# Router logits with the weights stationary: two 64-column halves and a product with unit matrices

## The reference

```python
xt = rmsnorm(h, norm2_g)
g_logits = xt @ w_rg + b_rg                 # 4 groups
g_w, g_idx = top_k(softmax(g_logits), 1)
e_logits = (xt @ w_rexp + b_rexp).reshape(-1, 4, 8)
e_w, e_idx = top_k(softmax(e_logits[group g_idx]), 2)
# every row is then sent to its two experts of 32 (gate, up, down) and the results are added to h
```

## Time and profile before

| what | value |
|---|---|
| median of 3 timed runs | 782.52 us |
| lowest and highest | 781.94 and 783.98 us |
| span of the profiled execution, first to last instruction | 783.6 us |
| busy share of PE, PEld | 95%, 74% |
| busy share of DVE, ACT, POOL | 52%, 33%, 9% |
| bytes read, written | 176.17 MB, 21.41 MB |
| mean granted clock of TensorE | 0.990 |

### The profile page before, as it was taken

One profiled execution on the slowest core, in us unless ns is written; L12 is line 12 of the kernel. 1 busy time (PEld: TensorE's weight loads), 2 busy tenths in 40 slices (PEclk: granted clock), 3 DMA queues, 4 the chain that ended last, 5 costly groups with the idle time before them and its releaser, 6 DMA issues.

```text
span 783.6 us, 12757 instructions
## 1 busy us (share of the span) xinstructions
PE 741.4 (95%) x5288; PEld 576.0 (74%) x5288; DVE 408.8 (52%) x755; ACT 259.2 (33%) x446; POOL 74.4 (9%) x104
## 2 busy tenths in 40 slices
PE   8999999999999999999999999999999997778884
PEld 7999999999999777899999988885333332323322
DVE  6999839986347785665154386554112111114226
ACT  5662351123486645532442341230111111100113
POOL 0100022001011111000000000011121221111100
PEclk9999999999999999999999999999999999999997
DMA  9578326434238433400260694389999999999994
GB/s 342 202 264 316 109 82 106 118 115 151 102 131 323 162 138 118 182 1 2 108 219 12 222 425 189 128 353 345 419 423 424 418 424 424 419 423 425 422 388 161
DMA packets 38143, 190.68 MB, mean 243 GB/s; under 512 B 5914, under 2 KB 7466, under 8 KB 21864
## 3 DMA queue, kind: packets, MB, share of 16 engines
q1 hardware_dynamic: 23696, 148.22, 47.8%
q0 software_dynamic: 11200, 34.98, 13.4%
q10 hardware_dynamic: 3184, 6.60, 2.3%
HBM read 176.17 MB, written 21.41 MB: 252 GB/s over the span
## 4 chain that ended last, share of the span: by engine, by line
PE 76%; DMA 14%; DVE 5%; ACT 3%; issue 1%; SPq 1%; DVEq 0%; ACTq 0%; POOLq 0%
PE ps L662 72%; DMA sb<-in_wexp 11%; PE ps L676 4%; DMA expert_rows<-sb 2%; DVE sb L2763 1%; DMA sb<-expert_rows 1%; DMA sb<-in_xT 1%; DVE sb L2298 1%; DVE sb L2284 1%; SPq L562 1%; ACT sb L1431 1%; ACT sb L1631 1%; DVE sb L2696 0%; ACT sb L1653 0%; ACT sb L1636 0%
## 5 line engine op out<-in xcount | busy, mean ns | idle before, releaser
L662 PE MATMUL ps<-sr 128*128 128x288 f32 (+3 forms) x2906 | 407.3, 300 | 3.5 <-DVE ps L2701 3.0
L662 PEld LDWEIGHTS ps<-sr 128*128 128x128 f32 (+1 forms) x2906 | 388.1, 188 | 18.6 <-issue 5.6
L662 PE MATMUL ps<-sb 128*64 128x512 f32 (+16 forms) x1984 | 296.9, 429 | 28.7 <-DMA sb<-in_wexp 18.1
L662 PEld LDWEIGHTS ps<-sb 128*64 128x64 f32 (+7 forms) x1984 | 148.0, 148 | 149.8 <-issue 124.7
L2632 DVE SCALAR_TENSOR_TENSOR sb<-sb,ps 128x256 f32<-128x256 f32 x16 | 6.7, 421 | 117.7 <-ACT sb L1830 117.7
L676 PEld LDWEIGHTS ps<-sb 128*128 128x128 f32 (+3 forms) x398 | 42.2, 140 | 31.0 <-issue 28.6
L676 PE MATMUL ps<-sb 128*128 128x128 f32 (+3 forms) x398 | 53.7, 273 | 2.3 <-issue 1.4
L2246 DVE TENSOR_TENSOR sr<-sb,sr 128x2048 fp32r<-128x2048 f32 (+1 forms) x17 | 39.3, 2320 | 29.1 <-ACT sr L1545 19.0
L2640 DVE COPY sb<-ps 128x1024 f32<-128x1024 f32 x15 | 18.4, 1225 | 54.5 <-PE ps L662 54.5
L1431 ACT ACTIVATE sb<-ps 128x576 f32<-128x576 f32 (+3 forms) x28 | 21.9, 783 | 67.4 <-PE ps L662 47.4
L2357 DVE SCALAR_TENSOR_TENSOR sb<-sb,ps 128x576 f32<-128x576 f32 x24 | 18.1, 753 | 46.5 <-PE ps L662 46.3
(11 more groups left out here) (291 smaller groups left out, 509.2 us busy)
## 6 DMA issues: line engine op xcount, KB each, us to landing
sb<-in_wexp SPq DMA_DIRECT2D x91, 1024.0 KB, 22.1
sb<-in_wstream SPq DMA_DIRECT2D x33, 1024.0 KB, 5.7
expert_rows<-sb ACTq DMA_DIRECT2D x1, 4608.0 KB, 24.9
sb<-in_mkT POOLq DMA_DIRECT2D x8, 512.0 KB, 7.7
sb<-in_mv POOLq DMA_DIRECT2D x8, 512.0 KB, 5.1
sb<-expert_rows SPq DMA_DIRECT2D x4, 1024.0 KB, 9.0
sb<-in_wexp SPq DMA_DIRECT2D x5, 768.0 KB, 25.4
sb<-in_x SPq DMA_DIRECT2D x4, 512.0 KB, 14.1
```

The lines of the kernel that those rows point to most:

```text
L662: return signed(nc.tensor.matmul(*a, **kw))
```

## The change

The operands of the logits change places. The router weights are stationary: padded from 40 to 64 columns a block, blocks of even number in the lower 64 columns of the array and of odd number in the upper 64, while the turned rows move (128 columns). The eight products of a tile so leave two partial sums, 64 partitions each, over the rows of the tile: job `lT`. ACT copies it to `M_LT` (`copy_lT`). A new PE step `logit_sums` multiplies it, as the stationary side, with two unit matrices set one over the other (`M_SUM`), which adds the halves and turns them back to rows by 40 columns: job `lg`, which DVE reads as before. `logit_sums(t-1)` stands one step into `w2t` (for tile 0 three steps into w31, for tile 4 three steps into `first_rows(1)`), and `ranks(0)` moves from behind w31 to two steps into w02. The job list has one job more a tile, so the PSUM buffers fall differently. `wr` grows from 368 to 560 columns and is loaded in two transfers; DVE builds `M_SUM` and scales 512 columns in place of 320.

```diff
-M_G2, M_WR, M_BR, M_GT = O_TH, O_TH + 2048, O_TH + 2368, O_TH + 2408
+M_G2, M_BR, M_GT = O_TH, O_TH + 2368, O_TH + 2408
+M_WR = O_TH + 1024
+M_LT = O_TH + 1536
+M_SUM = O_TH + 2048
...
-            jobs += ["w01", "w11", "x2T0", "w21", "lg0", "w31", "rk0"]
+            jobs += ["w01", "w11", "x2T0", "w21", "lT0", "lg0", "w31", "rk0"]
...
-        jobs += [f"x2T{t - 1}", f"w0{t}", f"tb{t - 2}", f"lg{t - 1}", f"w2{t}", f"rk{t - 1}"]
-    jobs += ["x2T4", "xs", "lg4", "tb3", "rk4", "xs2", "tb4", "cnt"]
+        jobs += [f"x2T{t - 1}", f"w0{t}", f"tb{t - 2}", f"lT{t - 1}", f"lg{t - 1}", f"w2{t}", f"rk{t - 1}"]
+    jobs += ["x2T4", "xs", "lT4", "tb3", "lg4", "xs2", "rk4", "tb4", "cnt"]
...
+                take(f"lT{t}")
+                for kt in range(0, KT, 2):
+                    for x in range(2):
+                        last = mm(pat(pair(f"lT{t}"), 0, (1, R), p0=64 * x, pn=64), at(M_WR + (kt + x) * 64, (1, 64)),
+                                  at(M_X2T + (t % 2) * 1024 + (kt + x) * 128, (1, R)), start=(kt == 0), stop=(kt == KT - 2))
+                last.then_inc(ps_ready, 1)
+
+            def logit_sums(t):
+
+                R = WROWS[t]
+                pe.wait_ge(lT_sb, t + 1)
                 take(f"lg{t}")
-                for kt in range(KT):
-                    last = mm(pat(pair(f"lg{t}"), 0, (1, 40), pn=R), at(M_X2T + (t % 2) * 1024 + kt * 128, (1, R)),
-                              at(M_WR + kt * 40, (1, 40)), start=(kt == 0), stop=(kt == KT - 1))
-                last.then_inc(ps_ready, 1)
+                mm(pat(pair(f"lg{t}"), 0, (1, 40), pn=R), at(M_LT + (t % 2) * 128, (1, R)), at(M_SUM, (1, 40)), start=True,
+                   stop=True).then_inc(ps_ready, 1)
...
+                    if b == 3 and kt == 3:
+                        logit_sums(0)
...
-            ranks(0)
...
+                        if t == 2 and b == 0 and kt == 2:
+                            ranks(0)
                         if b == 0 and kt == 5:
                             turn_norm(t - 1)
+                        if b == 2 and kt == 1:
+                            logit_sums(t - 1)
...
-            first_rows(1)
+            first_rows(1, range(3))
+            logit_sums(4)
+            first_rows(1, range(3, KT))
...
+            def copy_lT(t):
+                R = WROWS[t]
+                copy_out(f"lT{t}", at(M_LT + (t % 2) * 128, (1, R)), pat(pair(f"lT{t}"), 0, (1, R)), lT_sb)
...
                     copy_x2T(t - 1)
+                    copy_lT(t - 1)
...
+            copy_lT(4)
             act.wait_ge(rs_last, 1)
...
-            dve.wait_ge(ld["wr"], 16)
-            c.do(v.tensor_tensor(at(M_WR, (40, KT), (1, 40)), at(M_WR, (40, KT), (1, 40)), at(M_GT, (1, KT), (0, 40)),
+            dve.wait_ge(ld["wr"], 32)
+            op(v.tensor_tensor(at(M_SUM, (1, 40)), at(O_ID, (1, 40)), at(O_ID + 64, (1, 40)), ALU.add), False)
+            c.do(v.tensor_tensor(at(M_WR, (64, KT), (1, 64)), at(M_WR, (64, KT), (1, 64)), at(M_GT, (1, KT), (0, 64)),
                                  ALU.mult), wr_ready)
+            c.settle()
...
-                    pool.dma_start(at(M_WR, (1, 368)), wr).then_inc(ld["wr"], 16)
+                    pool.dma_start(at(M_WR, (1, 64 * KT)), wr[:, 0:64 * KT]).then_inc(ld["wr"], 16)
+                    pool.dma_start(at(M_BR, (1, 48)), wr[:, 64 * KT:64 * KT + 48]).then_inc(ld["wr"], 16)
```

More of the change, by code:

```diff
@@ L473, in build @@
         added, opened, seeded = (sem(n) for n in ("added", "opened", "seeded"))
-        out_st = sem("out_st")
+        out_st, lT_sb = sem("out_st"), sem("lT_sb")
         block = ctx.enter_context(nc.Block())
@@ L1176, in first_rows @@
                         last.then_inc(rows_ps, 1)
-                if t in (0, 3) and kts[-1] == KT - 1:
+                if t in (0, 2) and kts[-1] == KT - 1:
                     last.then_inc(ps_ready, 1)
@@ L3007 @@
     rows = cat([a["norm2_g"][0], a["final_norm_g"]])[None]
-    wr = cat([a["w_rg"][0], np.zeros((D, 4), f32), a["w_rexp"][0]], axis=1)
+    wr = cat([a["w_rg"][0], np.zeros((D, 4), f32), a["w_rexp"][0], np.zeros((D, 24), f32)], axis=1)
     wr_bias = cat([a["b_rg"][0], np.full(4, -3e38, f32), a["b_rexp"][0]])
-    wr = cat([columns_block(wr, ar(40)), tile(wr_bias, (P, 1)), a["norm2_g"][0].reshape(KT, P).T], axis=1)
+    wr = cat([columns_block(wr, ar(64)), tile(wr_bias, (P, 1)), a["norm2_g"][0].reshape(KT, P).T], axis=1)
     ins = dict(small=small, ssm=ssm, h0=h0, xT=xT, x=x, memT=memT, mem=a["mem_prompt"][0], wstream=wstream, wexp=wexp, bias=bias, sbias=sbias,
```

## The result

In 15 timed runs of each kernel in turn the changed kernel took 785.0 us in the median (783.95 to 787.56), the kernel before 783.64 (781.94 to 785.33): a ratio of 1.0021, 95% interval 1.0012 to 1.0031. The forecast was 779.7, with a range up to 782.5. So the change made the kernel slower by some 0.2%, less than the 0.3% set as the bound of "no change", but on the other side of what was forecast.

The account below looks back on a forecast made before the run. PE bounds the kernel up to about 542 us, then expert-weight transfers. PE saves 1.95 us plus 1.5 from the clock, some 3.45; 2.2 to 3.45 reaches the end, middle 2.8: 782.5 - 2.8 = 779.7, range 778.3 to 782.5.

Parts of the forecast that it names:

- From 542 us the end is therefore set by bytes: Expert stage: DMA engines full from 542 us at 420 GB/s, so PE's work between 542 and 639 is worth nothing.
- the end gains at least 0.85 + 1.3 = 2.2: End of kernel: chunks 11 to 18 start 0.85 us earlier, plus 1.3 us idle in the transfer gap; at most 3.45.
- the lower end of the forecast: End of kernel: the smallest gain forecast, 2.2 us, against a middle of 2.8 and at most 3.45.
- the rival of the unclosed gap: Transfers at 535 to 542: store, chunk 19 and gathers take as long as before; gain only 0.85, 781.7 us; chance 0.08.
- The eight products: Logits on PE: 16 instructions take 0.95 us, saving 0.8 for each tile of 128 rows, nothing for the 64-row tile.
- The sums: Product with unit matrices on PE, one more per tile: 0.18 to 0.27 us, taken as 0.25, five times.
- What a change of form may cost: PE switching between 64 and 128 columns: none charged; by the tiling-mode rule tile 0's sum would make the gain 1.1 smaller.
- ACT, DVE, POOL, PSUM turns: Around the logits: ACT's copy at most 0.38 us, hidden; PSUM turn covered by 0.5, DVE by 0.6; POOL's load free.
- The clock at 526: PE behind logits(4) and its table: the granted clock stays at 1.00 instead of falling to 0.50, worth 1.5 us.
- The base: Starting time: the profiled span of 783.6 us lies 1.1 above the timed median, so the gain is subtracted from 782.5.
- the rivals: Four: clock falls all the same 0.2; gap doesn't close 0.08; halves don't overlap 0.06; PE empties at each sum 0.06.
- The slower one: PE empties at both edges of every sum, 10 x 0.54 = 5.4 us, less 1.95: 3.45 more, 786; chance 0.06.

Follow-up runs that it names:

- e14: Changed kernel plus three unread products filling PE's gap ahead of turn_rows(1), the slot release left on turn_rows(1): 781.85 us, 0.998 of the kernel before.
- e4: Changed kernel with tile 4 in the old form, tiles 0 to 3 in the new: 782.37 us, 0.9982 of the kernel before.
- e10: Changed kernel with tile 4 in the old form, measured again on another chip: 781.51 us, 0.9979 of the kernel before.
- e9: The changed kernel itself, measured again as a control: 785.23 us, 1.0024 of the kernel before.
- e15: The changed kernel itself, measured as a control on another chip: 783.95 us, 0.9997 of the kernel before.
- e8: Changed kernel with the store of the last normalised rows issued by ACT instead of POOL: 785.41 us, 1.0006 of the kernel before.
- e3: Changed kernel with ten unread float32 products on PE ahead of gate_up(0,0), some 8.6 us: 788.25 us, 1.0062 of the kernel before.

## Why the prediction failed

**The step that failed** is the sentence "From 542 us the end is therefore set by bytes, and what happens to PE between 542 and 639 is worth nothing", and with it "the end gains at least 0.85 + 1.3 = 2.2". The first half held, the second did not follow: until some 555 us few chunks are in flight, each is released by an expert product, and when gate_up(1,0) is late by 2 us, the stream breaks (158 GB/s at 550 to 553). With the gather as late as ever and only PE's gap filled, so that the clock stays up (e14), the kernel is 2.1 us faster. I had counted one release, that of gate_up(0,0), and taken those behind it as given. From 484 to 542 the changed kernel moved 1.3 MB more than the kernel before, 0.93 MB of it in the closed gap alone (133 GB/s more for 7 us, 2.2 us at 420 GB/s: the lower end of the forecast). Behind 542 it lost 1.18 and 0.33 MB again, as two windows of the changed kernel

```profile
542.00:556.00 14.00, 12.34 (x50) 4.64 (x50) 0.42 (x1) 1.79 (x3) 1.00 (x1) 0.76 0.88 332
556.00:639.00 83.00, 83.00 (x400) 29.46 (x399) 14.05 (x20) 12.17 (x20) 14.23 (x14) 1.00 1.01 417
```

and of the kernel before show:

```profile
542.00:556.00 14.00, 12.89 (x68) 5.02 (x66) 1.75 (x5) 3.20 (x5) 0.99 (x1) 1.00 1.01 416
556.00:639.00 83.00, 83.00 (x404) 29.94 (x402) 14.46 (x21) 12.30 (x21) 14.18 (x14) 1.00 1.02 421
```

The price that was missing is that of the gather. The prediction listed the gathers only under the rival of the unclosed gap, and never asked when PE needs the first one. The rows to ask with were there: the gather of the kernel before landed at 541.4 and turn_rows(1) started at 543.40, a margin of 2.0 us, while the DMA engines, at a share of 0.81 from 535 to 542, were to be full around it. PE came 4.15 us sooner to the end of gate_up(0,1) (539.32 against 543.47) and the gather was asked for 3.48 us sooner, which alone would have left a margin; the 4.5 us by which the gather grew made the wait.

Step by step. Two points of the list rest on PE's rows at tile 0 in the changed kernel, the new halves of 64 rows and their sum within w31:

```profile
471.76 0.69 PE L665 MATMUL ps<-sb 128*64 128x64 f32 x16
472.38 1.33 PE L665 MATMUL ps<-sr 128*128 128x256 f32 x9
473.63 0.31 PE L665 MATMUL ps<-sb 128*64 128x40 f32 x2
473.87 3.42 PE L665 MATMUL ps<-sr 128*128 128x256 f32 x21
```

- *The eight products*: right, and too small. Tile 1's logits came out 0.79 us shorter ahead of the sum, with the table in front (1.38 against 2.17; 0.8 said); the tile of 64 rows, charged with no gain, takes 0.62 in place of 1.05 us of PE's time (471.76 to 472.38). turn_norm(4) starts at 519.24, 1.86 us earlier, where 1.4 was forecast, and chunk 11 goes out 1.20 us earlier (511.31), where 0.85 was.
- *The sums*: 0.23 us for the one at 484.90, against the 0.25 taken; 0.36 for that of tile 0, see below.
- *What a change of form may cost*: next to nothing, as charged. The edge that the prediction priced at 1.1 us is the sum of tile 0, 64 columns among 128. In the rows above, nine products at 0.126 end at 473.51 and the next starts at 473.87, so this sum costs 0.36 us, 0.11 more than was taken, and no idle time of PE is shown at either edge. The Trainium skill (TensorEngine Tiling (Array Packing), Key Properties) says that a change of tiling mode drains TensorE; a drain of 0.54 us an edge, as the prediction priced it, does not show here, and whether a short one is among the 0.11 can't be told.
- *ACT, DVE, POOL, PSUM turns*: covered, as said; PE shows no wait between 464 and 539 us.
- *The clock at 526*: it stayed at 1.00, as forecast, and place_rows(4) is 4.16 us earlier where 3.45 was forecast. The reason given is not borne out: with the old 40-column products kept for tile 4 (e4 and e10) the clock stayed at 1.00 in that stretch as well. So the forecast came true here by luck as far as the reason goes, and why the clock fell in the one trace of before is open.
- *The base*: 1.1 us was subtracted because the span stood 1.1 above the median and inside the spread of the timed runs. But a span is some 1.8 us less than a device time, so the profiled execution stands for 785.4 us, some 3 above that median and as long as the longest of the fifteen runs (785.33). Part of what I read in it need not be in every run, and the saving was reckoned from it. That the fall at 526 made it long is not shown: its mean clock, 0.990, is no lower than that of the other runs of the kernel (0.988 to 0.990 in the mean on each chip). Even without the wait the gain over before was 1.6 to 2.0 us (e4, e10 and e14 in medians), not 2.8; whether the base is the rest of it was not tested.

None of the rivals was it. The slower one put its price on PE's sums; what came was a wait for a transfer, 15 us behind the last of them (523.84). The three profiles of the same changed kernel differ in how long the clock stayed at 0.50 (1.2 GHz), by windows of 1 us: from 543.3 to 550.2, from 542.7 to 549.6 (e9), and only from 544.1 to 547.5 (e15). Why it does so stays open; the order of their spans (783.3, 783.1, 780.9) goes with the issue of chunk 24.

## What to carry to other kernels

When work ahead of a stream of loads gets faster, list every wait of the first turns of its ring, with the margin of each in the old trace, and ask what the earlier loads will do to the small transfers among them: "bound by bytes" begins only when enough loads are in flight that a late release costs nothing. A wait of PE is to be priced with the slower products behind it, and those with what they release. And an improvement that arrives all at once can be worth less than a part of it: here the change without its last tile beats both kernels (e10).

## What the runs showed of the hardware

- The first gather of rows took 3.5 us to landing in the kernel before, where 240 GB/s moved at 535 to 542, and 4.7 (266 GB/s) with chunk 20 held back, but 6.7 to 8.0 us with two 1 MB chunks issued from 1.3 to 1.5 us behind it on.
- In the four traces in which PE idled 2.36 to 3.23 us ahead of turn_rows(1), having run at 1.00, its clock was 0.57 to 0.79 in the mean of the 8 us from 542, and gate_up(1,0) took 5.35 to 6.50 in place of 3.65 us. The idle 1.11 us that all traces of the table have a little later, ahead of gate_up(1,0), had no such fall behind it where the first was absent, nor had a wait of 1.05 us for the rows followed by one of 1.11 in e8, where gate_up(1,0) took 3.65 us.
- A float32 product of 128x128 by 512 on the whole array cost some 0.87 us, two instructions (ten products took 8.76 us in e3); the 16 instructions of gate_up, on alternating halves with the same 512 columns, took 3.65, 0.23 each, at a clock of 1.00.
- Float32 products with 64 columns stationary on alternating halves and 64 moving cost 0.62 / 16 = 0.039 us an instruction, against 1.05 / 16 = 0.066 with 40 moving on one half.
